# Moving Pool out of a barrier, and the work on both sides of it, where a decoder's mLSTM stage meets its GLA stage

## What is computed

```
def _gla_core(seqs, s0):
    # S_t = diag(a_t) S_{t-1} + k_t v_t^T, o_t = S_t^T q_t
    b = jnp.cumsum(ac, axis=1)
    decay = jnp.exp(jnp.where(mask, b[:, :, None] - b[:, None], -jnp.inf))
    att = jnp.einsum('bthk,bshk,btshk->bhts', qc, kc, decay)
    o = jnp.einsum('bhts,bshv->bthv', att, vc) + jnp.einsum('bthk,bhkv->bthv', qc * jnp.exp(b), s)
    s = s * jnp.exp(bl)[..., None] + jnp.einsum('bshk,bshv->bhkv', kc * jnp.exp(bl[:, None] - b), vc)
...
o_gl = _head_rms(o_gl, p['gla_norm']) * jax.nn.silu(gg)
```

## Time and profile before

| what | value |
|---|---|
| median of 3 runs | 2383.44 us (2382.97 to 2386.2) |
| the profiled execution's own time | 2383.05 us |
| its span | 2381.5 us |
| mean granted TensorE clock | 0.963 of full |

### The profile page before, as it was taken

One profiled execution on the slowest core, in us unless ns is written; L12 is line 12 of the kernel. 1 busy time (PEld: TensorE's weight loads), 2 busy tenths in 40 slices (PEclk: granted clock), 3 DMA queues, 4 the chain that ended last, 5 costly groups with the idle time before them and its releaser, 6 DMA issues.

```text
span 2381.5 us, 34419 instructions
## 1 busy us (share of the span) xinstructions
PE 2200.2 (92%) x13669; PEld 2102.5 (88%) x13669; DVE 1169.3 (49%) x1973; ACT 669.7 (28%) x1071; POOL 181.6 (8%) x339
## 2 busy tenths in 40 slices
PE   4999978899999699999998688999999999999996
PEld 3988878899998699999998688999999999999995
DVE  6424421667675355445443477542222235555565
ACT  5123212233321233334331243010000013333342
POOL 1000011323130200000000111010000010000000
PEclk8989999899999799999999699999999999999998
DMA  4112154122211412111110455132111123111112
GB/s 171 48 43 66 60 72 134 54 79 65 83 59 50 114 49 63 51 45 48 45 53 19 156 183 194 44 137 90 53 44 44 44 100 137 44 35 44 44 44 83
DMA packets 82635, 178.27 MB, mean 75 GB/s; under 512 B 10465, under 2 KB 50097, under 8 KB 82321
## 3 DMA queue, kind: packets, MB, share of 16 engines
q1 hardware_dynamic: 67056, 123.35, 16.7%
q0 software_dynamic: 15488, 54.13, 7.0%
q10 hardware_dynamic: 32, 0.01, 0.0%
HBM read 129.43 MB, written 48.02 MB: 75 GB/s over the span
## 4 chain that ended last, share of the span: by engine, by line
PE 75%; DVE 12%; DMA 4%; ACT 4%; issue 3%; POOL 1%; DVEq 0%; POOLq 0%; ACTq 0%; SPq 0%
PE PS L453 19%; PE PS L454 19%; PE PS L455 18%; DMA AR<-zrows 2%; PE PS L955 2%; PE PS L1073 2%; PE PS L1069 2%; PE PS L1063 2%; DMA orows<-AR 1%; DVE AR L1871 1%; DVE AR L2236 1%; DVE AR L1869 1%; ACT AR L1376 1%; ACT AR L1406 1%; PE PS L1120 1%
## 5 line engine op out<-in xcount | busy, mean ns | idle before, releaser
L453 PE MATMUL PS<-HT_parts,W_parts 128*128 128x358 f32 x1440 | 512.5, 356 | 22.6 <-ACT AR L504 18.5
L454 PE MATMUL PS<-OT_parts,W_parts 128*128 128x358 f32 x1440 | 478.8, 332 | 0.0
L455 PE MATMUL PS<-HT_parts,W_parts 128*128 128x358 f32 x1440 | 477.1, 331 | 0.0
L453 PEld LDWEIGHTS PS<-HT_parts,W_parts 128*128 128x128 f32 x1440 | 279.4, 194 | 32.4 <-ACT AR L504 19.4
L454 PEld LDWEIGHTS PS<-OT_parts,W_parts 128*128 128x128 f32 x1440 | 279.2, 194 | 1.9
L455 PEld LDWEIGHTS PS<-HT_parts,W_parts 128*128 128x128 f32 x1440 | 278.3, 193 | 0.0
L453 PE MATMUL PS<-ACT_parts,CF_parts 128*128 128x358 f32 x768 | 255.4, 333 | 13.1 <-issue 7.6
L453 PE MATMUL PS<-HN_parts,CF_parts 128*128 128x358 f32 x768 | 250.6, 326 | 1.2 <-DVE OT_parts L535 1.2
L455 PE MATMUL PS<-ACT_parts,RING_parts 128*128 128x358 f32 x768 | 250.9, 327 | 0.0
L455 PE MATMUL PS<-HN_parts,RING_parts 128*128 128x358 f32 x768 | 250.4, 326 | 0.0
L454 PE MATMUL PS<-OT_parts,CF_parts 128*128 128x358 f32 x768 | 250.2, 326 | 0.0
(11 more groups left out here) (387 smaller groups left out, 3651.1 us busy)
## 6 DMA issues: line engine op xcount, KB each, us to landing
RING<-in_w_all SPq DMA_DIRECT2D x132, 512.0 KB, 3.7
zrows<-AR SPq DMA_DIRECT2D x162, 179.0 KB, 1.9
AR<-zrows POOLq DMA_DIRECT2D x32, 537.0 KB, 3.9
AR<-zrows SPq DMA_DIRECT2D x8, 640.0 KB, 4.5
AR<-in_xT SPq DMA_DIRECT2D x8, 537.0 KB, 7.0
HT<-in_xT POOLq DMA_DIRECT2D x8, 537.0 KB, 6.8
residual<-HT POOLq DMA_DIRECT2D x8, 537.0 KB, 6.6
acts<-AR POOLq DMA_DIRECT2D x8, 537.0 KB, 3.2
```

Source lines behind the costliest of these rows:

```text
L453: e.matmul(out, whi, xhi, start=first, stop=False)
L454: e.matmul(out, whi, xlo, start=False, stop=False)
L455: return e.matmul(out, wlo, xhi, start=False, stop=last)
```

## The change

Five things are done together.
1. **Pool leaves barrier 2**: `phase` has to reach 7 instead of 8 (and 11 and 15 later). The tiles that Pool still sends (SM, OTM, RM) now lie where GLA has only OTG and SG, and SyncE and Pool guard those two by waiting for `out` and `o_sent`.
2. **The engines arrive earlier**: TensorE after the last tile's output, with ten steps of its chunk left; ScalarE with that pair's second half to evacuate; VectorE before the low parts of (9, 0) and (9, 1). In every mLSTM tile the low part moves from the middle to the end.
3. **The first tile's rows, prelude, levels and exponentials** go ahead of pair J_GL0: SyncE issues `gl_rows(0)` before the pair's load and copies, TensorE the logits before its matmuls, and ScalarE runs prelude, one evacuation, exponentials, and then the other evacuations.
4. **Silu in place**: rows 12 and 13 are evacuated by Copy and get Silu as one instruction on OTG, after SyncE has read them back. Rows 14 and 15 are read by a copy of their own.
5. **In every GLA tile** the next tile's levels (VectorE) and exponentials (ScalarE) stand after its prelude. On ScalarE the pair's last evacuation, with the `weights_hi` behind it, comes after these exponentials.

```diff
-        RI, RF, RT, RB, RM = (a.take(rows=4, c=W) for _ in range(5))
+
+        SM = a.take(s=SEGS, c=260)
+        OTM = a.take(k=2, t=W)
+        RM = a.take(rows=4, c=W)
+        SENT_END = a.at
+        RI0 = a.at
+        RI, RF, RT, RB = (a.take(rows=4, c=W) for _ in range(4))
...
+        assert SENT_END <= GX0
...
-                e.wait_ge(S("phase"), 4 * k)
+                e.wait_ge(S("phase"), PHASES[k])
+
+        PHASES = {1: 4, 2: 7, 3: 11, 4: 15}
...
-            for u in range(2):
-                stream_sent(e, J_GL0, u)
-            e.wait_ge(S("phase"), 8)
+            e.wait_ge(S("phase"), PHASES[2])
...
             rows_sent(e, Z_QKV + 10)
             gl_rows(0, P)
             for u in range(2):
+                stream_sent(e, J_GL0, u)
+
+            e.wait_ge(S("out"), 14 * 16)
+            e.wait_ge(S("o_sent"), 2 * 16)
+            rows_sent(e, Z_OG + 2)
+            e.dma_start(OTG[:, 0:2], Z[Z_OG:Z_OG + 2].rearrange("r p t -> p r t")).then_inc(S("gl_gates"), 16)
+            for u in range(2):
                 stream_sent(e, J_GL0 + 1, u)
             rows_sent(e, Z_OG + 4)
-            e.dma_start(OTG, Z[Z_OG:Z_OG + 4].rearrange("r p t -> p r t")).then_inc(S("gl_gates"), 16)
+            e.dma_start(OTG[:, 2:4], Z[Z_OG + 2:Z_OG + 4].rearrange("r p t -> p r t")).then_inc(S("gl_gates"), 16)
...
-            barrier(e, 2)
+            e.wait_ge(S("phase"), PHASES[2])
...
-                rest(work)
+                if not last_tile:
+                    rest(work)
...
-            ml_tile(TILES, 0, LASTW, stream_pair(e, J_MLT), True)
+            work = stream_pair(e, J_MLT)
+            ml_tile(TILES, 0, LASTW, work, True)
             barrier(e, 2, False)
-
-            rest(stream_pair(e, J_GL0))
+            rest(work)
...
                 e.matmul(PS(2, 3 * P, 3 * P + w), WGA[0:16, :], GA[0:16, at], start=True, stop=True).then_inc(S("gl_z"), 1)
-            e.wait_ge(S("phase"), 8)
+            e.wait_ge(S("phase"), PHASES[2])
             gl_logits(0, P)
+            rest(stream_pair(e, J_GL0))
             rest(stream_pair(e, J_GL0 + 1))
...
-                if last_tile:
-                    evacs(3)
...
-            ml_tile(TILES, LASTW, J_MLT, (0, 1), 0)
-            barrier(e, 2)
-
-
-            def silu_pair(j):
-                for u in range(2):
-                    for g in range(3):
-                        stream_out(e, j, u, g, ACT.Silu)
-            silu_pair(J_GL0)
-            exp_ln_table(e)
+            ml_tile(TILES, LASTW, J_MLT, (0,), 0)
+            barrier(e, 2, False)
+            for g in range(3):
+                stream_out(e, J_MLT, 1, g)
+            e.wait_ge(S("phase"), PHASES[2])
...
+            def gl_exps(m, w):
+
+                x = GXL if w < P else GX
+                nl = len(LHALVES if w < P else HALVES)
+                b = GB[:, :, 0:w]
+                e.wait_ge(S("gl_b"), m + 1)
+                e.activation(x[:, :, 0, :], b, ACT.Exp)
+                if w == P:
+                    for g in range(3):
+                        e.activation(x[:, g, nl + 1, :], b[:, g], ACT.Exp, scale=-1.0, bias=b[:, g, P - 1:P])
+                e.wait_ge(S("x_ready"), m + (GL_N + 1))
+                hi = nl + 2 if w < P else nl + 1
+                e.activation(x[:, :, 1:hi, :], x[:, :, 1:hi, :], ACT.Exp).then_inc(S("x_exp"), 1)
             gl_prelude(0, P)
-            silu_pair(J_GL0 + 1)
+            stream_out(e, J_GL0, 0, 0)
+            gl_exps(0, P)
+            for u, g in ((0, 1), (0, 2), (1, 0), (1, 1), (1, 2)):
+                stream_out(e, J_GL0, u, g)
+
+            for u in range(2):
+                for g in range(3):
+                    stream_out(e, J_GL0 + 1, u, g, ACT.Silu)
+                if u == 0:
+                    e.wait_ge(S("gl_gates"), 16)
+                    e.activation(OTG[:, 0:2], OTG[:, 0:2], ACT.Silu)
             exp_ln_table(e)
...
-                b = GB[:, :, 0:w]
-                e.wait_ge(S("gl_b"), n + 1)
-                e.activation(x[:, :, 0, :], b, ACT.Exp)
-                if not last_tile:
-                    for g in range(3):
-                        e.activation(x[:, g, nl + 1, :], b[:, g], ACT.Exp, scale=-1.0, bias=b[:, g, P - 1:P])
-                e.wait_ge(S("x_ready"), n + (GL_N + 1))
-                hi = nl + 2 if last_tile else nl + 1
-                e.activation(x[:, :, 1:hi, :], x[:, :, 1:hi, :], ACT.Exp).then_inc(S("x_exp"), 1)
...
                 if w_next:
                     gl_prelude(n + 1, w_next)
-                evacs(4 if last_tile else 2)
+                    evacs(1)
+                    gl_exps(n + 1, w_next)
+                evacs(1 if w_next else 4)
...
-                weights_lo(e, *pairs[0])
+                for pair in pairs[:-1]:
+                    weights_lo(e, *pair)
...
-                for pair in pairs[1:]:
-                    weights_lo(e, *pair)
+                if not last_tile:
+                    weights_lo(e, *pairs[-1])
...
-            barrier(e, 2)
+            barrier(e, 2, False)
+            weights_lo(e, 9, 0)
+            weights_lo(e, 9, 1)
+            e.wait_ge(S("phase"), PHASES[2])
...
-            weights_lo(e, 9, 1)
-            weights_lo(e, 10, 0)
-            gl_prelude(0, P)
-            weights_lo(e, 10, 1)
-            weights_lo(e, 11, 0)
-            e.wait_ge(S("zeroed"), 2)
-            e.wait_ge(S("states_in"), (11 + 8) * 16)
-            e.wait_ge(S("gl_gates"), 16)
...
+            def gl_levels(m, w):
+
+                x = GXL if w < P else GX
+                halves = LHALVES if w < P else HALVES
                 b = GB[:, :, 0:w]
...
+            gl_prelude(0, P)
+            gl_levels(0, P)
+            for p, u in ((10, 0), (10, 1), (11, 0)):
+                weights_lo(e, p, u)
+            e.wait_ge(S("zeroed"), 2)
+            e.wait_ge(S("states_in"), (11 + 8) * 16)
+            e.wait_ge(S("gl_gates"), 32)
...
                 if w_next:
                     gl_prelude(n + 1, w_next)
+                    gl_levels(n + 1, w_next)
```

More of the change, by code:

```diff
@@ L266, in build @@
         M4 = a.take(s=6, t=W)
-        SM = a.take(s=SEGS, c=260)
         EMM = a.take(t=TILES + 1, h=4)
@@ L272, in build @@
         GST = a.take(rows=4, t=P)
-        MQH = Arena(KEEPTO, KEEPTO + W).take(h=4, t=P)
-        MX = Arena(KEEPTO + 2 * W, KEEPTO + 3 * W).take(h=4, t=P)
+        MQH = Arena(RI0, RI0 + W).take(h=4, t=P)
+        MX = Arena(RI0 + 2 * W, RI0 + 3 * W).take(h=4, t=P)
         MATT = a.take(h=4, t=P)
@@ L284, in build @@
         MSL = a.take(n=TILES)
-        OTM = a.take(k=2, t=W)
         a = Arena(KEEPTO, EARLY)
@@ L612, in sp_program @@
                 stream_sent(e, J_GLT, u)
-            e.wait_ge(S("phase"), 12)
+            e.wait_ge(S("phase"), PHASES[3])
             def rw_rows(n, w):
@@ L1858, in gl_tile, with tile_of @@
                     ins = e.tensor_tensor(half(o, h, True), bb[:, :, :, h:], mid, ALU.subtract)
-                if last_tile:
-                    for lo, hi, m in ((0, TAIL, TAIL), (TAIL, w, DSEQ)):
-                        o = x[:, :, nl + 1, lo:hi].rearrange("p g (n t) -> p g n t", t=m)
-                        bb = b[:, :, lo:hi].rearrange("p g (n t) -> p g n t", t=m)
-                        ins = e.tensor_tensor(o, bc(bb[:, :, :, m - 1:m], o.shape), bb, ALU.subtract)
-                ins.then_inc(S("x_ready"), 1)
+                if w < P:
+                    for lo, hi, n in ((0, TAIL, TAIL), (TAIL, w, DSEQ)):
+                        o = x[:, :, len(halves) + 1, lo:hi].rearrange("p g (n t) -> p g n t", t=n)
+                        bb = b[:, :, lo:hi].rearrange("p g (n t) -> p g n t", t=n)
+                        ins = e.tensor_tensor(o, bc(bb[:, :, :, n - 1:n], o.shape), bb, ALU.subtract)
+                ins.then_inc(S("x_ready"), 1)
+            gl_prelude(0, P)
[5 more added lines that the diff above has]
+            e.wait_ge(S("gl_gates"), 32)
+            def gl_tile(n, w, j, w_next):
+                last_tile = w < P
+                x, q = GXL if last_tile else GX, GE[:, :, 0:w]
+                halves = LHALVES if last_tile else HALVES
+                nl = len(halves)
+                qt, kt = ZT[:, 0:3, 0:w], ZT[:, 3:6, 0:w]
+                def tile_of(y):
+                    return y[:, TILES * P:NT] if last_tile else y[:, bass.ds(n * P, P)]
                 weights_lo(e, j + 3, 1)
```

12 lines of the change are left out of this document (1 added, 11 removed).

## The result

The changed kernel takes 2411.83 us (median of 5 runs, 2408.63 to 2414.49), the kernel before in the same comparison 2385.12 (2382.97 to 2387.34). The ratio is 1.0115, 95% interval 1.0101 to 1.0129: slower by 27 us, where 2384.0 and no measurable change were forecast. The profiled execution took 2408.63 us and has a span of 2407.1, 25.6 more than that of before; its mean granted clock is 0.957 where it was 0.963.

The account below looks back on a forecast made before the run. TensorE, busy 92% of the span, was taken as the bound, with DMA binding the stretch before GLA. Terms +1.6 - 11.8 + 11.2 = +1.0 us gave 2384.0 us; the forecast's own range 2378 to 2391, overall 2372 to 2393.

Parts of the forecast that it names:

- The start of GLA: Barrier into GLA: the rows' copy lands at 356.5, TensorE restarts at 360.4 instead of 356.70; +1.6 us in sum.
- Rival B: Start of GLA: the first tile's rows come early, so the start gives -5.8 us; 2376.6 us, chance 0.15.
- The first tile: First GLA tile: products and level 2 start 8.7 us earlier, and 3.1 us more from the clock; -11.8 us.
- The forecast's 4.8: First GLA tile: time in us taken for reading back half of OTG's bytes, half and 0.65 of latency.
- one of the ends given (-8): First GLA tile: -8 us if the half copy takes as long or the clock still falls; the other end -13.
- Every full tile: Seven later full GLA tiles: the late high part delays low part and products, 1.6 us a tile; +11.2 us.
- rival C: Full GLA tiles: the clock falls in the new waits, 3.1 us a fall; four of seven give 2396.4; chance 0.15.
- Rival A: Full GLA tiles: the low part doesn't hold the products, seven waits (6.7 us) go; -16.9, 2366 us; chance 0.10.

Follow-up runs that it names:

- 8: Experiment 1's kernel with all of Pool's outputs at mLSTM's end waiting until the first tile's rows are in SBUF: 2360.94 us, ratio 0.9911.
- 10: Experiment 1's kernel with only Pool's six outputs of 4-byte pieces waiting for the first tile's rows, the rest sent at once: 2363.24 us, ratio 0.9927.
- experiment 1: The changed kernel with both last evacuations, and the high part of weights, ahead of the next tile's exponentials in GLA tiles: 2368.27 us, ratio 0.9932.
- experiment 5: The changed kernel with Pool's spreading for level 3 starting only when VectorE has made all its products: 2402.86 us, ratio 1.0079.
- Experiment 4: The changed kernel with 18 unread matmuls per full GLA tile ahead of the level-2 wait for the diagonal: 2387.1 us, ratio 1.0021.
- experiment 7: Experiment 1's kernel with seven extra reductions per full tile on VectorE ahead of the diagonal: 2414.24 us, ratio 1.0142.
- 9: The changed kernel with VectorE's low part of (j + 3, 1) moved behind the diagonal select in GLA tiles: 2364.22 us, ratio 0.9937.
- 11: Experiment 8's kernel with VectorE's wait for OTG's read-back moved from ahead of the first tile to its product into OTG: 2355.17 us, ratio 0.9891.
- experiment 2: The changed kernel with parts 1 to 4 alone, later tiles' levels and exponentials at their own start as before: 2372.26 us, ratio 0.9951.
- 6: Experiment 1's kernel with three extra reductions per full tile on VectorE ahead of the diagonal: 2384.08 us, ratio 1.0012.
- 3: The kernel before with part 5 alone, the next tile's levels and exponentials after its prelude: 2417.21 us, ratio 1.0156.

## Why the prediction was wrong, point by point

**The start of GLA, right.** +1.6 was forecast: rows down at 356.5, a restart at 360.4 after a wait of about 12 us, and a second one of 1.0; less the 2.5 us by which this trace runs ahead, 354.0 and 357.9. Measured: rows at 354.1, restart at 357.98, waits of 11.90 and 1.30. That the DMA was the bound here and Pool's place in the barrier wasn't is what decided this step, and experiments 8 and 10 show which part of the DMA; Pool's place by itself had no run. Rival B (rows early) did not come. Its mechanism exists all the same: with the small stores away the rows land 4.7 us after their issue. The Trainium skill ("DMA: Bandwidth & Descriptors", "Queues, rings and completion order") has a DMA engine go round-robin, packet by packet, between the queues with work. Counted in the profile's packets, that is not what experiment 1's trace shows while the small stores are on their way (19 packets of SyncE's queue against 69 of Pool's between 340 and 345 us).

**The first tile, right but for the clock.** The wait of 7 us is gone. VectorE went on at 408.75, where 409.4 less 2.5 was forecast: the half of OTG read last was issued at 403.29 and took 5.1 us. The forecast's 4.8 contained 0.65 of latency that no row shows. TensorE waited 2.12 us before level 2 instead of 3.5. The step counted 3.1 us for the clock staying up from level 2 to the transposes. That stretch took 13.44 us, between the 15.0 of before and the 11.9 of the forecast, and the granted clock in it was 0.72 from 418 to 424. It was one of the ends given (-8).

**Every full tile, the step that failed.** The sum put the clock's fall behind the new waits at nothing, and left VectorE's products at their old length. The chain itself was right: the high part behind the exponentials makes the low part, the products and the diagonal late. The forecast was 1.6 us a tile; 5.2 were measured, made of three terms.
- The chain itself, 1.6: the products start 20.79 us after the last tile's transposes (452.53 - 431.74), in the kernel before 19.24 (501.53 - 482.29). The wait grew by 2.35 in all, of which this is what is left after the next term.
- Pool beside VectorE, 0.8: the later products now meet Pool's third spreading, which TensorE's first level releases. In experiment 5, where it starts later, they take 6.63 us instead of 7.26. The forecast took 6.44 as fixed, though the trace of before has products of 0.35, 0.56 and 0.79 us one beside the other, and the slow ones were those beside Pool. The Trainium skill ("Advanced Engine Details and Errata", "GPSIMD Details") says that Pool shares a read and a write interface with VectorE and conflicts with its instructions that have two SBUF inputs. The products have two, and the trace agrees.
- The clock, 2.8, the largest: rival C, seven times out of seven. Experiment 4 takes it away with the wait's cause still there, experiment 7 brings it back with that cause gone, at all seven waits.

C was priced at 3.1 us a fall and given a chance of 0.15, because the clock had stayed at 1.00 through a gap of 3 us at 383 and the new waits were to be 2.6. The waits became 3.3, but the argument did not fail by that: at 2.5 to 2.7 us (experiment 5) the clock fell as well. One gap survived was taken for a rule, against one that had not survived, at 777 in the same rows, and against the first tile of before, where the products behind waits of 7.01 and 2.40 us ran at the lower clock. Both stood in the forecast's own rows. With falls in all seven tiles the forecast's terms give 1.0 + 7 x 3.1 = 22.7 us; with Pool's 0.8 a tile 28.3. The spans differ by 25.6, the medians by 26.7. That this comes so near is in part luck: a fall cost 2.8 us and not 3.1, the start and the first tile gave 1.3 less than forecast, and 2.5 came from ahead of the stage.

**Rival A** (the low part does not hold the products) was rightly refused: it does. It also says roughly what the change could have been: 2366 was its time, and experiments 1 and 9 give 2368.27 and 2364.22. Its terms did not come out alike: of the 6.7 us of waiting in the full tiles, experiment 1 gains 3.8, since the clock falls in two tiles.

**What stays open.** Why a gap of 3 us at 383 us of the kernel before left the clock up, why it falls in two of seven tiles without a wait (experiments 1 and 8 to 11) and in none of the fourteen with waits of 0.9 to 1.0 us (the kernel before and experiment 2), and what decides at 1.45 us, is not settled; rows show when it fell, not why. What makes the traces differ ahead of mLSTM's end wasn't tried either.

## What to carry to other kernels

When an instruction is moved, follow what stands behind it on its engine and who waits for that: here exponentials moved ahead of one evacuation carried a weights split, a second engine's products and TensorE's wait with them. Price a new wait of TensorE that comes back in every tile with the slow stretch behind it: here 2.8 us at waits of 3.3 us, nearly as much on average at waits of 2.5 to 2.7, nothing at waits of 0.96. Where a long one can't be removed, work that fills it can pay, as 18 useless matmuls did. And look at small stores of 4-byte pieces next to a transfer that the path waits for: they can wait, it can't.

## What was not expected of the hardware

- Six stores in 4-byte pieces, 4.5 KB in all, held both DMA queues for some 10 us: the queue of SyncE moved 0.03 MB in 5 us with them and 1.19 MB without, and 537 KB of output landed 19.6 us after their issue with them and 3.9 without.
- 18 matmuls more in each tile (4) made the kernel 22 us faster than the changed one by the two ratios, 2.8 us a tile by the clock.
- Waits of TensorE ahead of the same product and the clock of the seven periods: under 0.1 us, 1.00 in five and 0.96 in two (experiments 1 and 8 to 11); 0.9 to 1.0, 1.00 in all (before and 2); 1.45, 0.96 in four (6); 2.5 to 2.7, 0.92 in five and 0.96 in two (5); 3.3, 0.92 in all (the changed kernel, 3 and 7). A short wait did no harm to the clock; having none did not keep it up.
